# Second transformer block, input projections: the mLSTM gate chain in five pieces, the head norms' squares behind each tile's emptying, and the sixteen gate rows split by GpSimd's transfers

## The reference

```
hl = rms_norm(xl, norm_mix) * (1.0 + sc1_l) + sh1_l          # hc likewise from xc
aq_l, ak_l, av_l, mq_l, mk_l, mv_l, mo_l, mg_l, pp_l = jnp.split(hl @ w_in, IN_OFFSETS, -1)
q_l = apply_rope(rms_norm(aq_l.reshape(B, T, ATT_HEADS, HEAD_DIM_2), q_norm), cos, sin)
k_l = apply_rope(rms_norm(ak_l.reshape(B, T, ATT_KV_HEADS, HEAD_DIM_2), k_norm), cos, sin)
...
att_l = block_attention(q_l, jnp.concatenate([k_l, k_c], 1), jnp.concatenate([v_l, v_c], 1))

def ml_gates(gp, n):
    return (gp + b_gates).astype(F32).reshape(B, n, 4, ML_HEADS).transpose(2, 0, 3, 1)
...
li, lf = g[2 * direc], jax.nn.log_sigmoid(g[2 * direc + 1])   # both directions, four heads
b = jnp.cumsum(lf, -1)                                        # and running maxima of li - b
```

## Time and profile before

| | |
|---|---|
| median of 3 runs | 2491.09 us (2489.82 to 2499.41) |
| the profiled execution | 2490.22 us, its span 2488.4 us |
| granted TensorE clock, mean over the span | 0.924 |
| PE busy | 2179.3 us, 88% |
| weight loads (PEld) | 1657.1 us, 67% |
| DVE busy | 1347.8 us, 54% |
| ACT busy | 903.2 us, 36% |
| POOL busy | 445.0 us, 18% |

### The profile page before, as it was taken

How to read it: one execution, slowest core, us unless ns; L and a number is a source line. 1 busy time by engine, 2 the same in 40 slices (tenths; PEclk the granted TensorE clock), 3 DMA queues, 4 the chain that set the end, 5 groups by cost and what they waited for, 6 DMA issues and landing times.

```text
span 2488.4 us, 33930 instructions
## 1 busy us (share of the span) xinstructions
PE 2179.3 (88%) x13589; PEld 1657.1 (67%) x13589; DVE 1347.8 (54%) x2633; ACT 903.2 (36%) x1779; POOL 445.0 (18%) x417
## 2 busy tenths in 40 slices
PE   6969897878989996899798976999999997878998
PEld 5847676647646695798453433678888864547998
DVE  4639676655578849454334456433333334455555
ACT  3325454542222273443222434222222212444443
POOL 0037969508911000000000000000000000000000
PEclk8989999989999998899899977899999998978999
DMA  8163545595687658865621312422323432224653
GB/s 276 57 204 108 168 122 143 163 275 180 213 268 219 193 197 320 232 170 181 192 68 51 102 35 87 131 93 86 96 81 93 115 102 85 85 81 140 196 162 118
DMA packets 434035, 366.34 MB, mean 147 GB/s; under 512 B 66238, under 2 KB 412622, under 8 KB 431702
## 3 DMA queue, kind: packets, MB, share of 16 engines
q1 hardware_dynamic: 392212, 320.87, 41.8%
q0 software_dynamic: 7424, 26.38, 2.9%
q10 hardware_dynamic: 34242, 16.92, 2.4%
HBM read 317.58 MB, written 54.92 MB: 150 GB/s over the span
## 4 chain that ended last, share of the span: by engine, by line
PE 68%; DVE 16%; ACT 6%; DMA 5%; POOL 2%; issue 2%; ACTq 1%; SPq 0%; DVEq 0%; POOLq 0%
PE ps L119 65%; DVE A L88 6%; PE ps L122 3%; ACT A L115 3%; POOL A L88 2%; DVE R L88 2%; DVE A L102 1%; DVE A L105 1%; DVE A L92 1%; DMA A<-btab 1%; DVE A L93 1%; DMA wbuf<-in_ada_w 1%; ACT A L116 1%; DVE A L96 1%; DMA xs<-X 1%
## 5 line engine op out<-in xcount | busy, mean ns | idle before, releaser
L119 PE MATMUL ps<-R,R 128*128 128x256 f32 (+1 forms) x3968 | 845.6, 335 | 35.5 <-ACT R L115 25.1
L119 PEld LDWEIGHTS ps<-R,R 128*128 128x128 f32 x3968 | 632.1, 193 | 109.6 <-ACT R L115 30.3
L119 PE MATMUL ps<-HR,R 128*128 128x512 f32 (+1 forms) x1984 | 556.8, 365 | 30.7 <-DVE R L88 20.5
L88 DVE TENSOR_TENSOR R<-wbuf,R 128x1024 fp32r<-128x1024 f32 (+2 forms) x304 | 349.5, 1158 | 350.6 <-ACT R L115 350.3
L119 PEld LDWEIGHTS ps<-HR,R 128*128 128x128 f32 x1984 | 358.1, 193 | 89.8 <-issue 23.8
L115 ACT ACTIVATE A<-ps 128x512 f32<-128x512 f32 (+4 forms) x400 | 210.2, 557 | 544.2 <-PE ps L119 400.0
L115 ACT ACTIVATE R<-wbuf 128x1024 fp32r<-128x1024 f32 (+2 forms) x304 | 270.1, 894 | 281.8 <-PE ps L119 255.6
L88 DVE TENSOR_TENSOR A<-A 128x128 f32<-128x128 f32 (+4 forms) x868 | 321.7, 402 | 87.9 <-ACT A L115 58.5
L119 PE MATMUL ps<-H,wbuf 128*128 128x512 f32 (+2 forms) x928 | 336.1, 519 | 13.5 <-DVE H L93 13.4
L119 PE MATMUL ps<-A 128*128 128x64 f32 (+11 forms) x1896 | 292.5, 355 | 27.2 <-DVE A L88 7.7
L88 POOL TENSOR_TENSOR A<-A 128x512 f32<-128x512 f32 (+3 forms) x186 | 218.0, 1184 | 522.2 <-DVE A L96 260.6
(11 more groups left out here) (114 smaller groups left out, 1630.6 us busy)
## 6 DMA issues: line engine op xcount, KB each, us to landing
wbuf<-in_w_ada SPq DMA_DIRECT2D x48, 1024.0 KB, 5.2
wbuf<-in_ada_w SPq DMA_DIRECT2D x24, 1024.0 KB, 8.8
wbuf<-in_w_out SPq DMA_DIRECT2D x24, 1024.0 KB, 5.6
wbuf<-in_w_ffn_gate SPq DMA_DIRECT2D x22, 1024.0 KB, 5.3
wbuf<-in_w_ffn_up SPq DMA_DIRECT2D x22, 1024.0 KB, 5.4
wbuf<-in_w_ffn_down SPq DMA_DIRECT2D x32, 704.0 KB, 4.7
wbuf<-in_attn_w_in SPq DMA_DIRECT2D x20, 1024.0 KB, 7.0
ctab<-A ACTq DMA_DIRECT2D x64, 256.0 KB, 2.8
```

The source lines that it names most:

```text
L88: return self.op(lambda e: e.tensor_tensor(out, a, b, op))
L119: return self.op(lambda e: e.matmul(out, lhsT, rhs, start=start, stop=stop, skip_group_check=True))
```

## The change

- `HeadNorm.act` is split: `squares` holds the square, `act` only the root. `flow` calls `squares` for both key tiles directly behind `Keys`, and for each q tile directly behind that tile's step of `lq`. In the mLSTM's output norms the two are still called together.
- `Gates` becomes five pieces. Piece 1, behind `kn[1]`: the panel's load, the 16-row product, its copy on ACT, and on POOL four DMAs that move four rows each to partitions 0 to 3 of `GT`. Piece 2, behind `kr[1]`: the four biases on DVE, now in SBUF. Piece 3, behind `pp`: direction 0 on ACT (Abs, Exp, Ln) and DVE. Piece 4, behind q1's step and square: direction 1 on ACT and DVE. Piece 5, behind q2's: the two last Exps on ACT.
- The four products with the unit matrix and their four PSUM tiles are gone. `G16` lies in q3's place instead of q0's.
- `GateColumns`, `qn[3]` and `qr[2]` stand behind the first `lqm` tile instead of the second.

```
         class Gates:
             def sp(self, sp):
                 load_panel(sp, (N, "gw"), W, 0, 8, 1792, 16, (mm_done, (N, "g16")))
+                yield
...
                 x.then_inc(mm_done, (N, "g16"))
-                pe.wait_ge(act_evac, (N, "g16"))
+                yield
+
+            def pool(self, pool):
+                pool.wait_ge(act_evac, (N, "g16"))
                 for gi in range(4):
-                    p = PS.take(pe, (N, "g", gi), (dve_evac, (N, "g", gi)))
-                    pe.mm(p[0:4, :], ident[0:16, 4 * gi:4 * gi + 4], G16, True, True).then_inc(mm_done, (N, "g", gi))
+                    pool.dma(GT[gi][0:4, :], G16[4 * gi:4 * gi + 4, :]).then_inc(l_gt, "g")
+                yield
...
             def dve(self, dve):
+                yield
+                dve.wait_ge(l_gt, "g")
+                dve.wait_ge(l_bg, "b")
                 for gi in range(4):
-                    dve.wait_ge(mm_done, (N, "g", gi))
-                    dve.wait_ge(l_bg, "b")
-                    dve.ts(GT[gi][0:4, :], PS[N, "g", gi][0:4, :], bg[:, l, gi:gi + 1], None, ADD
-                           ).then_inc(dve_evac, (N, "g", gi))
+                    dve.ts(GT[gi][0:4, :], GT[gi][0:4, :], bg[:, l, gi:gi + 1], None, ADD).then_inc(dve_evac, (N, "g", gi))
+                yield
...
             on(Keys())
+            squares(kn[0])
+            squares(kn[1])
             on(va)
             on(kn[0])
             on(kn[1])
+            step(gates)
             on(vm)
             on(kr[0])
             on(kr[1])
+            step(gates)
             on(pp)
-            on(Gates())
+            step(gates)
             gq = on(lq)
             for m in range(4):
                 step(gq)
+                squares(qn[m])
+                if m == 1 or m == 2:
+                    step(gates)
                 if m:
                     on(qn[m - 1])
                 if m > 1:
                     on(qr[m - 2])
-            rest(on(lqm))
+            qm = on(lqm)
+            step(qm)
             on(GateColumns())
             on(qn[3])
             on(qr[2])
+            rest(qm)
             rest(on(lkm))
```

More of the change, by code:

```diff
@@ L2259, in __init__ @@
         SEL = take(768)
-        l_rope, l_band, l_tri, l_sel, l_pw = [landing(f"{x}{l}") for x in ("rope2", "band", "tri", "sel", "pool_w")]
+        l_rope, l_band, l_tri, l_sel, l_pw, l_gt = [landing(f"{x}{l}") for x in (
+            "rope2", "band", "tri", "sel", "pool_w", "gate_rows")]
         x_ready = None
@@ L2359, in __init__, with squares @@
                 self.name, self.dst, self.raw, self.c, self.vcol, self.ready = name, dst, raw, c, vcol, ready
-            def act(self, act):
+            def squares(self, act):
                 c, key = self.c, (self.name, "hq")
@@ L2365, in act @@
                 act.act(rb[:, c:512], self.raw, ACT.Square).then_inc(act_step, key)
-                rsqrt_act(act, rb[:, c:512], (self.name, "hr"))
+            def act(self, act):
+                rsqrt_act(act, RO[self.name, "hq"][:, self.c:512], (self.name, "hr"))
             def pe(self, pe):
@@ L2422, in __init__ @@
         zero4, tmp4 = sc4[4][0:4, :], sc4[5][0:4, :]
-        G16 = QS[0:16, 0, :]
+        G16 = QS[0:16, 3, :]
         class Gates:
@@ L2435, in pe @@
                 for k in range(8):
+                    for s, key in h_ready(k):
+                        pe.wait_ge(s, key)
                     x = pe.mm(p[0:16, :], v[:, k, :], H[:, k, :], k == 0, k == 7)
                 x.then_inc(mm_done, (N, "g16"))
-                pe.wait_ge(act_evac, (N, "g16"))
+                yield
+            def pool(self, pool):
+                pool.wait_ge(act_evac, (N, "g16"))
                 for gi in range(4):
-                    p = PS.take(pe, (N, "g", gi), (dve_evac, (N, "g", gi)))
-                    pe.mm(p[0:4, :], ident[0:16, 4 * gi:4 * gi + 4], G16, True, True).then_inc(mm_done, (N, "g", gi))
+                    pool.dma(GT[gi][0:4, :], G16[4 * gi:4 * gi + 4, :]).then_inc(l_gt, "g")
+                yield
             def act(self, act):
@@ L2454, in act @@
                     act.act(tmp4, tmp4, ACT.Ln, bias=1.0).then_inc(act_step, (N, "ln", d))
+                    yield
+                for d in range(2):
                     act.wait_ge(dve_step, (N, "em", d))
                     act.act(EM[d], EM[d], ACT.Exp).then_inc(act_step, (N, "em", d))
+                yield
             def dve(self, dve):
+                yield
+                dve.wait_ge(l_gt, "g")
+                dve.wait_ge(l_bg, "b")
                 for gi in range(4):
-                    dve.wait_ge(mm_done, (N, "g", gi))
-                    dve.wait_ge(l_bg, "b")
-                    dve.ts(GT[gi][0:4, :], PS[N, "g", gi][0:4, :], bg[:, l, gi:gi + 1], None, ADD
-                           ).then_inc(dve_evac, (N, "g", gi))
+                    dve.ts(GT[gi][0:4, :], GT[gi][0:4, :], bg[:, l, gi:gi + 1], None, ADD).then_inc(dve_evac, (N, "g", gi))
+                yield
                 dve.wait_ge(pool_step, (N, "zero"))
@@ L2770, in act @@
                     if n - 4 in close_at:
+                        hm_norm[close_at[n - 4]].squares(act)
                         hm_norm[close_at[n - 4]].act(act)
@@ L2873, in act @@
             def act(self, act):
+                hm_norm[self.a].squares(act)
                 hm_norm[self.a].act(act)
@@ L2959, in flow, with squares @@
             step(backlog, 3 - l)
+            gates = on(Gates())
+            def squares(norm):
+                if e.name == "act":
+                    norm.squares(e)
             on(Keys())
+            squares(kn[0])
+            squares(kn[1])
             on(va)
```

## The result

| | before | after |
|---|---|---|
| median | 2495.25 us (2489.82 to 2501.87, 4 runs) | 2463.13 us (2454.28 to 2469.61, 4 runs) |
| ratio, 95% interval | | 0.9875 [0.9843, 0.9907] |
| profiled execution (its span) | 2490.22 us (2488.4) | 2454.28 us (2452.4) |
| granted clock, mean | 0.924 | 0.927 |
| PE, ACT, POOL busy | 2179.3, 903.2, 445.0 us | 2160.2, 906.5, 449.5 us |

The forecast was 2460.8 us (2451 to 2471): the median lies 2.3 us above it, inside the range. That it lies so near is in part luck, since two misses offset each other: the base of 2490.22 us was one execution, 5.0 us under the median of the four, and the gain by the medians is 32.1 us instead of 29.4.

A forecast was written before the change was run, and what follows sets the result against it. TensorE's chain of waits (68% held by PE), its idle time released by ACT and low clock, was taken as the bound; 12.5 + 1.8 + 11.2 + 3.9 = 29.4 us off 2490.2 gave 2460.8 us, range 2451 to 2471.

The forecast's parts named there:

- Part 1: Key squares, `va` to `vm`: PE's waits and slow start of `vm` go, 4.2 + 0.7 us; block 1 3.3 + 1.8.
- Part 2, the size: Sixteen gate rows, ahead of q0: waits and 4-row products go, 5.8 us, slow passes 1.8; block 1 4.2 and 1.9.
- Part 2, the reason: Slow q0 and q1 passes vanish because the clock was 1.00 in the 16-row product, falling only among 4-row ones.
- The transfers: POOL's four SBUF-to-SBUF DMAs ahead of the biases: landing in about nothing to 8.3 us, free under 16.2 us cover (block 1).
- Rival (d): Transfers land late, DVE waits ahead of the biases; no gain left at 38 us, slower by 12.5 at 45; chance 0.05.
- Part 3, the wait: q0's rope product on PE waits for q0's norm behind direction 1: 8.5 us, block 1 10.2 us.
- T + 17.2: Block 0: start of q0's rope product, 17.2 us after T, the end of q1's passes.
- Part 3, the clock behind it: Low clock after q0's rope product's new wait costs 2.5 us, block 1 2.8; bounds 1 and 4.5 per block.
- rival (c): The new wait costs less, clock rising at once or never falling, 1.7 to 2.7 us per block; about 2454 us; chance 0.07.
- 16 us more: Sign expected in the changed profile: attention starts 14 us earlier in block 0 and 16 us more in block 1.

The follow-up runs named there:

- Squares alone: Kernel before the change with only the squares split off and placed directly behind each tile's emptying, gate chain whole in its old place: 2471.51 us, ratio 0.9921 to before.
- Experiment 4: Changed kernel, but four 4-row products on PE behind the key ropes split the sixteen rows instead of transfers: 2480.19 us, ratio 0.9949 to before.
- experiment 5: Against rows split by PE: 4-row products and biases directly behind the 16-row product, 2468.59 us; same with the 16-row product issued twice, 2482.48 us.
- the early directions: Changed kernel with gate direction 0 ahead of `pp`, direction 1 behind it, last Exps behind `qn[3]` and `qr[2]`: 2439.09 us, ratio 0.9785; repeated 2445.58 us, 0.9826.
- experiment 6: Changed kernel with the four row DMAs issued by SyncE (SP) behind the gate panel's load instead of by GpSimd: 2461.89 us, one execution.

## Why the prediction was right, and where not

- **Part 1**, 4.2 + 0.7 and 3.3 + 1.8: `va` to the 16-row product now holds 1.81 us of head sums and no wait; `vm` takes 14.08 with its row's end. Squares alone gave no wait there either. Right.
- **Part 2, the size**: 5.8 + 1.8 and 4.2 + 1.9 went, `q0` follows `pp` directly at 13.90. Right.
- **Part 2, the reason**: the failed step is "I let this go too, since the clock was still 1.00 in the 16-row product and fell only among the 4-row ones". From it I expected 4-row products to pull the clock down wherever they stand. Experiment 4 shows them at 1.00 in both blocks, experiment 5 shows the clock falling in three blocks of four where they stand directly behind the 16-row product. So pulling the two apart is enough for the clock's share of part 2, by whatever engine the rows are moved; why the pair lowers the clock stays open. With both on PE and apart, 3.7 of 7.6 us are gained in block 0 and 2.2 of 6.1 in block 1. The term came out right, and by luck as far as its reason goes: the transfers happened to take the pair apart.
- **The transfers**: free, as said. Bounds of nothing to 8.3 us for the landing; it took 4.1 us (4.3 in block 1). The Trainium skill (DMA: Bandwidth & Descriptors, "Anatomy of one DMA") fits about 2.0 us, and little more for 8 KB, for one transfer of GpSimd; the rows here show twice that for four issued in a row. Rival (d) needed 38 us.
- **Part 3, the wait**: 8.5 and 10.2 forecast, 8.60 and 10.09 measured (8.59 and 10.09, once 10.08, in the six other executions that keep this order). A chain added up from single rows of the old trace, handovers among them, held to 0.1 us, because ACT and DVE ran the same operations in a new order. T + 17.2 was exact. The rows show 1.28 us for a table load and 0.02 to the next activation again (1298.65 and 1299.95). The drain that the Trainium skill adds to a table load (ScalarE: Activation LUTs, "What ACT_TABLE_LOAD costs") would by estimate have made it T + 20.0; the trace doesn't show it.
- **Part 3, the clock behind it**: 2.5 and 2.8 forecast, measured 1323.18 - 1314.00 - 7.4 = 1.8 and 2070.52 - 2064.60 - 3.9 = 2.0. Mis-sized by 0.7 and 0.8 us, within its bounds, in the direction of rival (c). In block 0 this is most of the difference between 14.3 us forecast and 15.3 measured.
- **Block 1**: 17.4 us against 15.1 (the "16 us more" among the prediction's signs doesn't fit its own sum; the profile shows 28.3 - 13.4 = 14.9 us). Besides that 0.8, the sum took off only q1's head sum behind 2092.95 and left in the waits of 0.87 and 0.28 us that the early squares remove as well: 1.15 us that block 0's sum had counted. The rest is a few tenths in each direction.
- **Outside the stages**: -3.2 us in the profiled execution, not in the next one. It brought the profiled time to 2454.3 while the median agrees with the stages: 2495.25 - 32.8 = 2462.5.

Not tried: one DMA for all sixteen rows, and the early directions with the rows moved by PE.

## What to carry to other kernels

A new wait can be priced before it exists: lay the late engine's rows end to end from the last common point, handovers included, and subtract what the waiting engine has to do. Where a long chain of two slow engines (here 4 partitions wide) must be done sometime, look for the longest stretch of the bounding engine that needs neither of them; here the early squares and the chain in pieces together gave 32 us, and moving both directions ahead of the query tiles' norms another 18 to 22. When a term is right, its reason isn't yet: put the suspected instruction alone in another place before it is told on.

## What the runs showed of the hardware that was not expected

- Products with 4 output rows directly behind one with 16 were followed by a granted clock of 0.50 for some microseconds in 7 of 8 blocks, with PE busy throughout in one of them. 13.9 us of products with 16 rows alone weren't (2 blocks), and the 4-row products behind the ropes weren't (2 blocks).
- DVE's operation with two SBUF inputs on 128 x 512 took 1.79 us instead of 0.75 in block 0, where it lay beside the last of GpSimd's DMA issues and the whole of its first cosine product (1.80 in the five other executions with this order there, 0.75 with the DMAs on SP and that product out of the way). In block 1 it began 0.5 us before the last issue ended and took 1.19 us, and the two cosine products 1.96 instead of 1.42. A cosine product alone is enough to stretch such an operation (experiment 6); what the issuing adds isn't separated. The Trainium skill (GPSIMD Engine Reference, Specifications) says that GpSimd's SBUF interface is contended by VectorE instructions with two SBUF inputs; the rows agree, and VectorE pays, up to 1.0 us. Nothing waited for it here.
- Issuing four 8 KB transfers took 1.99 us of POOL's time and 2.64 us of SP's (2.47 in block 1).
